# Reordering the mixer's tokens by column octets in a two-block fp32 network

## What is computed

```python
def hybrid_mixer(u, w_in, rpb, pool_w, pool_scale, w_br_attn, w_br_pool, w_out):
    proj = u @ w_in
    q, k, v, xp, g_attn, g_pool = jnp.split(proj, splits, axis=-1)
    y_attn = neighbourhood_attention(q, k, v, rpb) @ w_br_attn
    y_pool = multiscale_pool(xp, pool_w, pool_scale) @ w_br_pool
    merged = jax.nn.sigmoid(g_attn) * y_attn + jax.nn.sigmoid(g_pool) * y_pool
    return merged @ w_out
```

## Time and profile before

| | |
|---|---|
| median of 3 runs | 2432.93 us (2431.61 to 2433.4) |
| profiled execution, its time | 2435.46 us |
| its span on the core | 2433.6 us |
| PE busy | 2292.3 us, 94% |
| DVE, ACT, POOL busy | 935.7, 736.7, 889.6 us |
| grid attention, from its slot 0 to the first matmul of the next block | 1640.95 to 1784.32 us |

### The profile page before, as it was taken

One profiled execution on the slowest core, in us unless ns is written; L12 is line 12 of the kernel. 1 busy time (PEld: TensorE's weight loads), 2 busy tenths in 40 slices (PEclk: granted clock), 3 DMA queues, 4 the chain that ended last, 5 costly groups with the idle time before them and its releaser, 6 DMA issues. The chain is left out here.

```text
span 2433.6 us, 28231 instructions
## 1 busy us (share of the span) xinstructions
PE 2292.3 (94%) x11512; PEld 1897.4 (78%) x11512; DVE 935.7 (38%) x1639; ACT 736.7 (30%) x1080; POOL 889.6 (37%) x704
## 2 busy tenths in 40 slices
PE   6999998999899999999899999999989999999997
PEld 6788896777788888677688888876677788888876
DVE  2164554433536365442531222454341352222252
ACT  3412214344221313434332221234322242122233
POOL 6532422212341433112145444452124435354432
PEclk9999999999999999999999999999999999999999
DMA  5321211102231212111123332232123213232321
GB/s 206 130 70 47 77 62 63 63 18 70 79 104 35 87 54 73 39 59 52 61 71 121 105 103 95 88 108 66 53 72 106 87 61 113 86 118 90 104 69 70
DMA packets 99809, 196.76 MB, mean 81 GB/s; under 512 B 3936, under 2 KB 16608, under 8 KB 99424
## 3 DMA queue, kind: packets, MB, share of 16 engines
q1 hardware_dynamic: 94416, 179.97, 22.4%
q10 hardware_dynamic: 5264, 14.98, 1.8%
HBM read 192.83 MB, written 2.10 MB: 80 GB/s over the span
## 5 line engine op out<-in xcount | busy, mean ns | idle before, releaser
L655 POOL TENSOR_TENSOR wl<-raw,wh 128x512 fp32r<-128x512 f32 (+2 forms) x700 | 889.4, 1303 | 1506.3 <-ACT wh L922 1506.3
L922 ACT CAST wh<-raw 128x2048 fp32r<-128x2048 f32 (+2 forms) x178 | 319.3, 1794 | 924.5 <-PE ps L702 788.3
L700 PE MATMUL ps<-xh,wh 128*128 128x512 f32 (+1 forms) x1280 | 482.8, 377 | 26.7 <-DVE xl L1252 15.3
L702 PE MATMUL ps<-xh,wl 128*128 128x512 f32 (+1 forms) x1280 | 474.6, 371 | 0.0
L701 PE MATMUL ps<-xl,wh 128*128 128x512 f32 (+1 forms) x1280 | 474.0, 370 | 0.0
L700 PE MATMUL ps<-wh,xh 128*128 128x512 f32 (+1 forms) x768 | 308.4, 402 | 6.9 <-ACT work L945 3.2
L701 PE MATMUL ps<-wl,xh 128*128 128x512 f32 (+1 forms) x768 | 301.5, 393 | 0.0
L702 PE MATMUL ps<-wh,xl 128*128 128x512 f32 (+1 forms) x768 | 300.8, 392 | 0.0
L700 PEld LDWEIGHTS ps<-xh,wh 128*128 128x128 f32 x1280 | 244.2, 191 | 70.5 <-issue 21.5
L702 PEld LDWEIGHTS ps<-xh,wl 128*128 128x128 f32 x1280 | 244.0, 191 | 40.8
L701 PEld LDWEIGHTS ps<-xl,wh 128*128 128x128 f32 x1280 | 244.4, 191 | 38.1
(11 more groups left out here) (203 smaller groups left out, 2542.7 us busy)
## 6 DMA issues: line engine op xcount, KB each, us to landing
raw<-w_in SPq DMA_DIRECT2D x56, 1024.0 KB, 5.1
raw<-w_out SPq DMA_DIRECT2D x20, 1024.0 KB, 4.9
raw<-f1g SPq DMA_DIRECT2D x10, 1024.0 KB, 5.0
raw<-f1u SPq DMA_DIRECT2D x10, 1024.0 KB, 4.9
raw<-f1d SPq DMA_DIRECT2D x10, 1024.0 KB, 4.9
raw<-f2g SPq DMA_DIRECT2D x10, 1024.0 KB, 4.9
raw<-f2u SPq DMA_DIRECT2D x10, 1024.0 KB, 4.9
raw<-f2d SPq DMA_DIRECT2D x10, 1024.0 KB, 4.9
```

Source lines behind the costliest of these rows:

```text
L655: pool.tensor_tensor(wl[s], raw[:, u % 2, k, 0:b.width], wh[s].bitcast(F32), ALU.subtract).then_inc(low_done, 1)
L700: pe.matmul(o, still[0], move[0], start=k0 + k == 0, stop=False)
L702: mm = pe.matmul(o, still[1], move[0], start=False, stop=k0 + k == b.ktiles - 1)
L922: act.copy(wh[:, u % 3, 0:nk, 0:b.width], raw[:, u % 2, 0:nk, 0:b.width]).then_inc(high_done, 1)
```

## The change

**Order of the tokens.** From the mixer's input to its output projection, a token's place is (octet of columns, row, column in the octet), where it was (row, column). A tile of 128 places then holds two neighbouring octets, all eight rows. The queries are stored with the first 64 places repeated at the end and are read from place 64 on, so that a tile of queries is two octets shifted by one against the tiles of keys. Its windows lie within two tiles of keys instead of four. The norm and the transposes write the places directly: `act.copy` and `dve.tensor_tensor` with octet patterns, in the norm two half-size instructions where there was one.

**Grid attention.** One phase of 16 items (`grid_order`), each a pair of heads and one query tile. Scores are four float32 matmuls of 128 columns, of 64 rows each, to banks 4 and 5 (one bank for each head, not doubled). The exponent's scale 0.125 moves to the evacuation of the queries, the mask into the bias table. DVE has one instruction for bias and minimum of the negated scores (`tensor_tensor_reduce`) for each head, and multiplies the exponentials by the inverse sums before PE transposes them, so PE's transposes now wait for DVE. The values are the stationary operand, 128 wide with the other head's half set to zero, so the output lands transposed in bank 7, a bank for four items. The 16 transposes, the second phase and the late evacuation go. Twelve pieces instead of sixteen lie inside the phase, in 15 slots.

**Pool.** The window sums of the four groups are taken together where they are the same; the mean's factor is an immediate, and the 16 edge tokens are corrected from a small table already loaded. The `inv_count` load goes, and the matmul of `pool` permutes from token order to places. `xp` no longer lies in the attention's memory.

**Weights, in the whole kernel.** A unit's cast is four instructions of one tile each, and POOL waits tile by tile.

```diff
-                pool.wait_ge(high_done, u + 1)
                 for k in range(nk):
+                    pool.wait_ge(high_done, tiles_upto[u] + k + 1)
...
-                act.copy(wh[:, u % 3, 0:nk, 0:b.width], raw[:, u % 2, 0:nk, 0:b.width]).then_inc(high_done, 1)
+                for k in range(nk):
+                    act.copy(wh[:, u % 3, k, 0:b.width], raw[:, u % 2, k, 0:b.width]).then_inc(high_done, 1)
```

```diff
-        pool_in = blk2(1536, "tr", "copy_pad", "act", xp, late=True)
-        add(Load((na_mask, na_mask_in), *((t, rpb_in[:, n].rearrange("p (h m j) -> p h m j", h=2, m=14))
-                                          for n, t in enumerate(bias_t))))
-        add(blk2(1024, "nat", "copy", "dve", NV))
-        add(blk2(512, "tr", "copy", "dve", NK[:, 0:2, :], 256))
-        add(Phase("na_bias", dve=1))
-        add(blk2(0, "tr", "copy", "act", NQ[:, 0:2, :], 256))
-        for half in range(2):
-            more = [pool_in] if half else [blk2(256, "tr", "copy", "act", NQ[:, 2:4, :], 256),
-                                           blk2(768, "tr", "copy", "dve", NK[:, 2:4, :], 256)]
-            grid = attend("grid", 4, 4 * half, 0)
-            beside(more, (grid, 8))
-            add(grid)
-        transpose(G2, 4, "y", None)
-        add(Late(pool_in))
-        add(Load((pw, pool_w), (inv_count, inv_count_in)))
+        add(Load(*((t, rpb_in[:, n].rearrange("p (h k) -> p h k", h=8)) for n, t in enumerate(bias_t))))
+        add(blk2(512, "tr", "copy", "dve", NK))
+        add(Phase("zero_values", dve=1))
+        add(blk2(1024, "nat", "heads_apart", "dve", NV))
+        add(blk2(0, "tr", "eighth", "act", NQ[:, 0:2, :], 256))
+        more_queries = blk2(256, "tr", "eighth", "act", NQ[:, 2:4, :], 256)
+        order, _ = grid_order()
+        grid = Phase("grid", *(len(o) for o in order), slots=17, writes="y")
+        grid.more_queries = more_queries
+        beside([more_queries, blk2(1536, "tr", "copy_pad", "act", xp)], (grid, 12))
+        add(grid)
+        add(Load((pw, pool_w)))
         add(Phase("windows", dve=1))
```

DVE in the new phase (`m` for an item's bias and minimum, `r` for its inverse sums), and PE's values:

```diff
+                        if kind == "m":
+                            dve.wait_ge(pe_step, e.pe + pe_at["s", n])
+                            pair, b = n // 4, n % 4
+                            for h in range(2):
+                                ins = dve.tensor_tensor_reduce(
+                                    out=n_prob[:, n % 2, 256 * h:256 * h + 256],
+                                    in0=ps[:, 4 + h, 0:256],
+                                    in1=bias_t[b // 3][:, 2 * pair + h, :], scale=-1.0, scalar=3e38,
+                                    op0=ALU.add, op1=ALU.min, accum_out=stat[:, 2 * n + h:2 * n + h + 1])
+                        elif kind == "r":
+                            dve.wait_ge(act_step, e.act + act_at["e", n])
+                            link(dve.reciprocal(stat[:, 64 + 2 * n:66 + 2 * n], stat[:, 32 + 2 * n:34 + 2 * n]))
+                            for h in range(2):
+                                pr = n_prob[:, n % 2, 256 * h:256 * h + 256]
+                                ins = dve.tensor_scalar(pr, pr, stat[:, 64 + 2 * n + h:65 + 2 * n + h], None, ALU.mult)
...
+                            for i in range(4):
+                                mm = pe.matmul(ps[:, 7, b * P:(b + 1) * P], NV[:, (b + i % 2) % 4, 2 * pair + i // 2, :],
+                                               n_prob_t[:, n % 2, i * P:(i + 1) * P], start=i == 0, stop=i == 3)
```

More of the change, by code:

```diff
@@ L151, in pipeline, with grid_order @@
     return tuple({s: i + 1 for i, s in enumerate(order)} for order in (pe, act, dve))
+def grid_order():
+    n = 16
+    pe = [("s", 0), ("s", 1)]
+    for k in range(n):
+        pe.append(("t", k))
+        if k + 2 < n:
+            pe.append(("s", k + 2))
+        if k:
+            pe.append(("v", k - 1))
+    pe.append(("v", n - 1))
+    act = [("e", 0)]
+    for k in range(n):
+        if k + 1 < n:
+            act.append(("e", k + 1))
+        act.append(("c", k))
+        if k and k % 4 == 0:
+            act.append(("h", k // 4 - 1))
+    act.append(("h", 3))
+    dve = [("m", 0)]
+    for k in range(n):
+        if k + 1 < n:
+            dve.append(("m", k + 1))
+        dve.append(("r", k))
+        if k > 4 and k % 4 == 1:
+            dve.append(("l", k // 4 - 1))
+    dve.append(("l", 3))
+    return (pe, act, dve), [{x: i + 1 for i, x in enumerate(order)} for order in (pe, act, dve)]
 def norm_order(first, pre, turned):
@@ L699, in piece @@
                         o = ps[:, b.bank(j), tokens]
+                        if half is not None and b.by_columns:
+                            move = [octets(w[:, k0 + k, :])[:, :, 32 * half:32 * half + 32] for w in (oh, ol)]
+                            o = octets(ps[:, b.bank(j), :])[:, :, 32 * half:32 * half + 32]
                     pe.matmul(o, still[0], move[0], start=k0 + k == 0, stop=False)
@@ L714, in run_slot @@
             def run_slot(e, n):
-                split = e.kind == "attend"
+                split = e.kind in ("attend", "grid")
                 for m, pc in enumerate(e.slots[n]):
@@ L1125, in _ @@
                                        scale=col("pool_scale", g)).then_inc(act_step, 1)
-                if e.kind not in ("attend", "level", "norm"):
+                if e.kind not in ("attend", "level", "norm", "grid"):
                     read_slot(e, 0)
```

288 lines of the change are left out of this document (182 added, 106 removed).

## The result

The changed kernel takes **2373.59 us** as the median of four runs (2370.64 to 2379.0), the kernel before 2433.16 on the same chip (2431.61 to 2436.04). The ratio is 0.9756, with a 95% interval of 0.974 to 0.9773: 59.6 us, where 60.1 were forecast. The profiled execution has a time of 2374.91 us and a span of 2373.0.

The account below looks back on a forecast made before the run. PE, busy 94% of the span, was taken as the bound. Savings 54.8 + 5.3 + 0.5 + 1.5 less costs 1.1, 0.6 and 0.3 gave 60.1 us, from 2432.9 to 2373 us; range 2364 to 2392.

Parts of the forecast that it names:

- Transposes, values, projections, half clock after the fill: PE in grid attention: 0.53 and 0.91 us an item, 1.47 or 2.83 for projections; 2.7 us at half clock once.
- Scores: Grid attention, PE: eight records of 128 columns at 0.108 us, taken as 0.95 an item; fourteen in the loop, 13.3 us.
- Fill: Start of the grid attention, first scores to first transposes: one fill of 5.6 us, with DVE's `m` at 1.1.
- Waits in the loop: PE waiting for DVE at the grid attention's transposes: an allowance of 1.5 us, with 0.3 us margin in short slots.
- the tail's half clock: First 17 matmuls of the block behind the grid attention: their 2.9 us lost at half clock go.
- The pool sums: DVE behind the grid attention: start 4.6 us after it, take 10.5 to 14.8; PE's wait and half clock go, 5.3 us.
- Rival 2: The pool sums still come too late, with a wait before `w_ba`: +5 us, 2378; chance 0.09.
- The lock: DVE and GpSimd's exclusive port pair exposes the loop's two added multiplications; at worst in every item, PE waits 15 us.
- Additions: Costs added: keys' block +1.1 us, norm's last tile +0.6, scattered writes +0.3; loads, mask and zeroing -0.5.
- rival 4: Scattered patterns slow the keys' half-width matmuls to half-clock pace: +19 us, 2392; chance 0.03.
- Casts: Four casts a unit let POOL start 1.3 us earlier, mostly helping the kernel's start: -1.5 us (+1 to -3).
- Rivals 3 and 5: 3: weight loading paces short matmuls, +20 us, 2393, chance 0.04. 5: split casts land on PE's path, 2453, chance 0.01.

Follow-up runs that it names:

- e12: The changed kernel run once more, as it is, without any change; 2372.67 us, ratio 0.9746 to the kernel before.
- e7: The changed kernel with the scores of both heads of a pair worked out from rows 0 to 63; 2382.34 us.
- e5: The changed kernel with POOL working out the low parts of seven units of weights for 8 of 512 columns alone; 2365.13 us.
- e11b: The changed kernel with three more DVE copies of 256 columns from PSUM in each grid attention item, ahead of the reductions; 2377.33 us.
- e4: The changed kernel with ACT's evacuation of the first gate block no longer waiting for the phases ahead of it; 2366.24 us.
- e1: The changed kernel with one cast for each unit of weights, as in the kernel before; 2377.89 us.

## Why the prediction was right, point by point

The total was met within 0.6 us, but that close by luck: two errors of four microseconds lay against each other, and a third term was too small. Of the prediction's own signs one failed, since there was to be no wait before the attention branch, and one was met by a hair: an item's steps were 0.53, 0.65 and 0.92, in sum 0.29 us less than forecast, where more than 0.3 was to count as wrong.

- **Transposes, values, projections, half clock after the fill**: 0.53, 0.91, 1.47 and 2.83 were forecast; 0.53, 0.92, 1.47 and 2.85 are in the trace, and 2.7 us at half clock for 2.7. The last is the profiled execution's; in e12 the same item takes 5.61 us, which leaves 1.6 at half clock.
- **Scores**: the step that took 0.95 us from the pace of single records was wrong. 0.65 was measured, 14 x 0.30 = 4.2 us too much in the sum. I had counted eight records as a chain; e7 shows that a pair of heads on the two halves of the rows overlaps.
- **Fill**: 5.10 us for 5.6. `m` took 0.78 us for 1.1: of the accumulator reads, estimated at 0.15 each, the first lies beside the next reduction and the second cost 0.08.
- **Waits in the loop**: an allowance of 1.5 us; measured were two waits, 1.94 us idle and 2.2 lost, both from multiplications beside POOL (e5). The cover was 0.6 us, not 0.3 (e11b), since `m` was shorter.
- Together 76.4 us for 80.6, and **the tail's half clock** went as forecast, 2.87 us for 2.9 (6.83 - 3.96).
- **The pool sums**: the step that failed. That they start 4.6 us behind the phase held (4.73). Their length of 10.5 to 14.8 us did not: 17.4, because the stretching of the old ones was carried over in proportion, where it comes by the instruction, and the added short instructions were caught too (e4, e5). 1.2 of the 5.3 us came, and 4.1 stayed (2.5 in e12, whose matmuls behind the wait ran at full clock). Of those 1.2 most belong to the split casts: with one cast the wait is 3.47 us (e1). Rival 2 had this mechanism right, and with it alone the time would have been its 2378.
- **The lock**: the Trainium skill (SBUF — State Buffer, section SBUF: two separate sides) was weighed at the multiplications, and the trace agrees there: 346 to 355 ns with POOL idle, up to 1400 with POOL at work, while the reductions from PSUM stayed at 418 to 425. I did not apply the same rule to the pool sums, all of which have two inputs in SBUF; by it a 16-element step waits as long as a long one, and the measured 1.14 against 0.17 agrees with that too.
- **Additions**: keys, norm and scattered writes less the loads were 1.5 us together; for the mixer's stretch the forecast without the casts was 54.8 + 5.3 + 0.5 - 1.1 - 0.6 - 0.3 = 58.6. Measured with one cast on both sides, 330.15 - 272.40 = 57.8, and with split casts on both sides 325.95 - 268.80 or 267.62 = 57.2 or 58.3. The keys' matmuls of 256 scattered columns run at 0.120 (1602.16 - 1601.92 for two), as the contiguous ones of the earlier trace rows: rival 4 falls. The rule on non-contiguous patterns (the Trainium skill, Advanced Engine Details and Errata, section Memory Cachelines) finds no support here: these matmuls write PSUM in runs of 32 columns out of 64. The matmuls of `pool` read their moving operand from SBUF in runs of eight columns now, and take 3.67 us as before. PE's rows in the changed kernel, and last that of the kernel before:

```profile
1601.92 0.28 PE L753 MATMUL ps<-xl,wh 128*128 128x256 f32 x1
...
1602.16 0.29 PE L752 MATMUL ps<-xh,wh 128*128 128x256 f32 x1
...
1798.97 3.67 PE L991 MATMUL ps<-work 128*128 128x512 f32 x8 [0.98 <-DVE side L1295]
...
1859.33 3.67 PE L901 MATMUL ps<-work 128*128 128x512 f32 x8 [0.98 <-DVE side L1178]
```

- **Casts**: the sign was right and the size, 1.5 us, too small: 2.3 in the kernel before, 4.3 in the changed one. The term left out two things that the rows of the kernel before could have shown: that POOL's earlier start meets DVE's multiplications in the latent turns (a loss of some 3.4 on average), and that it also comes earlier where it gains, up to the end of the mixer (some 4, of which part is the clock's).
- **Rivals 3 and 5**: no sign of either. The short matmuls went faster than their pace, and PE waits for POOL once, 0.3 us in all, where it was six times.

## What to carry to other kernels

Price an elementwise instruction from SBUF to SBUF that may meet POOL at work per instruction, not per element: here about 1.0 us each, whatever its length, so many short SBUF-to-SBUF steps are the worst form beside it. When a faster or earlier step moves another engine's work (here POOL behind the split casts), look at every place where that engine now falls on someone's critical chain, not only at the place that it was meant for. And before a wait is put down to an engine, look whether that engine was done long ago: the wait before `w_ba` was for neither ACT's nor PE's work but for DVE's pool sums, by a conservative order that one condition lifted.

## What was not expected of the hardware

- Two float32 matmuls of 64 rows on different halves of the rows overlap: 0.65 us for eight records of 128 columns, against 1.09 on the same half, in either order of issue.
- On the same half, eight records with 64 rows take 0.136 us each, more than the 0.108 of the earlier trace rows with 128 rows. Why is open.
- DVE's read of an accumulator took 0.08 us and cost nothing beyond the pitch of 0.35 us between two reductions.
- The clock behind an idle time is not the same from one execution to the next: with 2.43 us idle at 372 us, the 16 transposes took 1.94 us in one execution of the changed program's code and 2.40 or 3.39 in others. What decides it is open; it moves a single execution by several microseconds.
